# A gated DeltaNet's decay sums and key scales: as rows that a DMA spreads over the partitions, in place of a product and transposes on TensorE

## The reference

```python
gc = jnp.cumsum(g.reshape(B, N, C, H).transpose(0, 3, 1, 2), axis=-1)
decay = jnp.exp(jnp.where(incl, gc[..., :, None] - gc[..., None, :], -jnp.inf))
M = jnp.where(strict, jnp.einsum('bhncd,bhnjd->bhncj', kb, kc) * decay, 0.0)
A = jnp.eye(C, dtype=jnp.float32) + M
uw = lax.linalg.triangular_solve(A, rhs, left_side=True, lower=True, unit_diagonal=True)
qk = jnp.einsum('bhncd,bhnjd->bhncj', qc, kc) * decay
```

## Time and profile before

| | us |
|---|---|
| median of three runs | 1629.28 |
| lowest, highest | 1624.13, 1629.74 |
| the profiled execution's own time | 1627.18 |
| its span, first to last instruction | 1625.4 |
| PE busy in the span | 1592.6 (98%) |
| PE weight loads | 1327.0 (82%) |
| DVE busy | 883.1 (54%) |
| POOL busy | 648.7 (40%) |
| ACT busy | 578.5 (36%) |
| DMA, mean | 118 GB/s |
| share of PE in the chain that ended last | 91% |

### The profile page before, as it was taken

One profiled execution on the slowest core, in us unless ns is written; L12 is line 12 of the kernel. 1 busy time (PEld: TensorE's weight loads), 2 busy tenths in 40 slices (PEclk: granted clock), 3 DMA queues, 4 the chain that ended last, 5 costly groups with the idle time before them and its releaser, 6 DMA issues.

```text
span 1625.4 us, 20530 instructions
## 1 busy us (share of the span) xinstructions
PE 1592.6 (98%) x7955; PEld 1327.0 (82%) x7955; DVE 883.1 (54%) x1326; ACT 578.5 (36%) x838; POOL 648.7 (40%) x477
## 2 busy tenths in 40 slices
PE   7999999999999999999999999999999999999998
PEld 4888888888888888888788887788888888878886
DVE  5322222454536353566554148756666565878886
ACT  4422221123222243333222134444444444444445
POOL 3334322312131223224324347987788888000111
PEclk9999999999999999999999999999999999999999
DMA  5232332121213042335367031422234433686575
GB/s 171 66 94 88 115 97 61 43 69 39 69 38 81 27 125 71 99 113 154 122 209 269 14 110 35 135 91 91 91 98 122 124 108 94 232 306 218 195 263 183
DMA packets 204172, 192.24 MB, mean 118 GB/s; under 512 B 23364, under 2 KB 156972, under 8 KB 204076
## 3 DMA queue, kind: packets, MB, share of 16 engines
q1 hardware_dynamic: 203856, 190.85, 37.8%
q10 hardware_dynamic: 220, 0.09, 0.0%
HBM read 142.57 MB, written 48.33 MB: 117 GB/s over the span
## 4 chain that ended last, share of the span: by engine, by line
PE 91%; DVE 4%; DMA 2%; issue 1%; POOL 1%; SPq 1%; ACT 0%; DVEq 0%; ACTq 0%
PE acc L562 37%; PE acc L2469 12%; PE bank_ab L1408 7%; PE bank_ab L2469 6%; PE acc L2479 6%; PE att_ps L2469 5%; PE att_ps L2479 3%; PE bank_ab L2479 3%; PE acc L1843 3%; PE att_ps L1483 2%; PE bank_ab L1843 1%; PE att_ps L1843 1%; PE att_ps L1465 1%; DVE u_t_full L1799 1%; PE att_ps L1476 1%
## 5 line engine op out<-in xcount | busy, mean ns | idle before, releaser
L562 PE MATMUL acc<-xh,w_high 128*128 128x512 f32 x832 | 276.9, 409 | 0.6 <-POOL xl L1732 0.6
L562 PE MATMUL acc<-xl,w_high 128*128 128x512 f32 x832 | 262.1, 392 | 0.0
L562 PE MATMUL acc<-xh,w_low 128*128 128x512 f32 x832 | 261.1, 390 | 0.0
L973 POOL TENSOR_TENSOR w_low<-w_raw,w_high 128x1024 fp32r<-128x1024 f32 x49 | 117.4, 2395 | 346.8 <-ACT w_high L1055 346.8
L562 PEld LDWEIGHTS acc<-xh,w_low 128*128 128x128 f32 x832 | 156.5, 188 | 34.2
L562 PEld LDWEIGHTS acc<-xl,w_high 128*128 128x128 f32 x832 | 156.6, 188 | 33.9
L562 PEld LDWEIGHTS acc<-xh,w_high 128*128 128x128 f32 x832 | 147.2, 189 | 27.0 <-issue 3.8
L1146 ACT ACTIVATE sc<-sc,mx 128x128 f32<-128x128 f32 (+1 forms) x96 | 35.5, 441 | 173.4 <-DVE mx L1352 173.4
L1246 DVE SCALAR_TENSOR_TENSOR cs<-acc,prm,cs 128x1023 f32<-128x1023 f32 (+2 forms) x36 | 46.1, 1281 | 77.0 <-ACT cs L1073 76.2
L2245 POOL TENSOR_TENSOR f_h<-f_h,f_fw 128x512 f32<-128x512 f32 x8 | 10.9, 1368 | 175.1 <-ACT f_junk L2168 175.1
L2479 PE MATMUL acc<-f_w_high,f_gh 128*128 128x512 f32 x176 | 69.6, 395 | 3.5 <-DVE f_gl L2333 3.5
(11 more groups left out here) (386 smaller groups left out, 3828.1 us busy)
## 6 DMA issues: line engine op xcount, KB each, us to landing
w_raw<-in_w_in_dram SPq DMA_DIRECT2D x51, 512.0 KB, 4.6
f_raw<-glu_d SPq DMA_DIRECT2D x66, 256.0 KB, 3.1
f_raw<-in_w_down_dram SPq DMA_DIRECT2D x55, 256.0 KB, 4.0
w_raw<-in_w_up_dram SPq DMA_DIRECT2D x24, 512.0 KB, 5.2
glu_d<-u_free_high SPq DMA_DIRECT2D x22, 512.0 KB, 4.6
u_raw_even<-in_w_up_dram SPq DMA_DIRECT2D x20, 512.0 KB, 4.7
f_raw<-gsum_d SPq DMA_DIRECT2D x33, 256.0 KB, 3.5
conv_d<-so SPq DMA_DIRECT2D x16, 512.0 KB, 3.0
```

The source lines that it names most:

```text
L562: mm = nc.tensor.matmul(out[:, lo:hi], w, xx[:, lo:hi], start=first and j == 0, stop=last and j == 2)
L973: g.tensor_tensor(wl[:, n % 2], raw[:, n % 2], wh[:, n % 2].bitcast(F32), ALU.subtract).then_inc(s_wlo, 1)
```

## The change

The running sums and the factors `nbr` are made once for all chunks as rows: 32 partitions (chunk and head) by 128 positions. They are written to HBM (`rows_d`), and for each chunk one DMA reads them back with the same 1024 numbers to all 128 partitions (`spread`, 512 KB). With these rows the factor along the free axis is a plain multiply, so `kT` (PE and ACT) is gone, and `XB` is made from the keys as they were loaded; the decay exponent is mask minus row (POOL), plus a column that ACT adds as its bias, so the product with `Ls` and POOL's masking are gone. ACT's one exponential of 128x512 becomes four of 128x128, one for each head's bias. The sums count from the middle of the chunk (`Um`: minus one in the upper left), so no exponent grows large. Everything else stays in its place: where `kT` stood there is a `rest`.

```diff
 def dn_stages():
     def front(c):
-        return [[(name, c)] for name in ("kt", "kT", "kkD")]
+        return [[(name, c)] for name in ("kt", "kkD")]
...
-        out += [("vq", c)] + kt + [("P4", c)] + kT + [("T4", c)] + kkD + rest + [("P5", c)] + ml + [("T5", c)] + ob + sv0
+        out += [("vq", c)] + kt + [("P4", c)] + rest + [("T4", c)] + kkD + rest + [("P5", c)] + ml + [("T5", c)] + ob + sv0
...
+            if kind == "conv" and t == 3 * NH - 1 and k == 4:
+                items.append(("rowsT",))
...
-    use_b = {"kkD", "vq", "T4", "T5", "T6", "kS", "so"}
+    use_b = {"vq", "T4", "T5", "T6", "kS", "so"}
... SP
+            def load_spread(c):
+                if c:
+                    sp.wait_ge(s_gu, 2 * c - 1)
+                    sp.wait_ge(s_a, a_taken[("kt", c - 1)])
+                sp.dma_start(spread, rows_d[:, c, :].rearrange("j (h t) -> j h t", h=NH).unsqueeze(0)
+                             .to_broadcast([P, 2, NH, P])).then_inc(s_rl, 16)
+                if kind == "rowsT":
+                    sp.wait_ge(s_attk, att_no[("gatesum",)])
+                    sp.wait_ge(s_attk, att_no[it])
+                    for j in range(2):
+                        sp.dma_start(rows_d[j].rearrange("c (h t) -> (c h) t", t=P), rows_t[j][0:NT * NH, :]
+                                     ).then_inc(s_rst, 16)
                     if name == "load":
+                        sp.wait_ge(s_rst, 48)
+                        load_spread(0)
... (kkD, behind the eight stores of WT)
+                        if c + 1 < NT:
+                            load_spread(c + 1)
... POOL
+            step(g.tensor_copy(Um[:], U[:]))
+            step(g.tensor_scalar(Um[0:P // 2, :], U[0:P // 2, :], -1.0, None, ALU.add))
                     if name == "kt":
-                        g.tensor_tensor(DTr[:], bh(U[:]), bc(g_all[:, c, :]), ALU.mult).then_inc(s_gu, 1)
+                        g.tensor_tensor(DTr[:], bh(amask[:, 0:P]), spread[:, 0], ALU.subtract).then_inc(s_gu, 1)
                     if name == "kkD":
-                        pool.wait_ge(s_b, b_taken[(name, c)])
-                        g.tensor_tensor(DTr[:], DTr[:], bh(U[:]), ALU.mult).then_inc(s_dtm, 1)
-                        pool.wait_ge(s_dtm, 2 * c + 1)
+                        pool.wait_ge(s_gu, 2 * c + 2)
                         g.tensor_tensor(DTr[:], DTr[:], bc(rr[:, 1, :, c]), ALU.mult).then_inc(s_dtm, 1)
... ACT
                 if kind == "gatesum":
+                    g.activation(g_all[:].rearrange("p c h -> p (c h)"), att0[:, 3 * NT * NH:4 * NT * NH], ACT.Copy, scale=-1.0)
+                    g.activation(rows_t[0][0:NT * NH, :], att0[0:NT * NH, P:2 * P], ACT.Copy, scale=-1.0)
+                if kind == "rowsT":
+                    g.activation(rows_t[1][0:NT * NH, :], att0[0:NT * NH, 0:P], ACT.Copy).then_inc(s_attk, 1)
-                    if name == "kT":
-                        g.activation(XB[:], A4, ACT.Copy).then_inc(s_a, 1)
                     if name == "kkD":
-                        g.activation(DTr[:], B4, ACT.Exp).then_inc(s_b, 1)
+                        act.wait_ge(s_gu, 2 * c + 1)
+                        for h in range(NH):
+                            ins = g.activation(DTr[:, h, :], DTr[:, h, :], ACT.Exp, bias=g_all[:, c, h:h + 1])
+                        ins.then_inc(s_gu, 1)
... DVE
-                        g.tensor_tensor(XB[:], A4, bc(nbr[:, c, :]), ALU.mult)
+                        dve.wait_ge(s_rl, 16 * (c + 2))
+                        g.tensor_tensor(XB[:], ckqk[c % 2][:, NH:2 * NH, :], spread[:, 1], ALU.mult)
... PE
-                    for j, m in enumerate((U, Ls, ones)):
+                    for j, m in enumerate((U, Ls, ones, Um)):
+                    last = t_.matmul(att0[0:NT * NH, P:2 * P], g_all[:].rearrange("p c h -> p (c h)"), Um[:],
+                                     start=True, stop=True)
+                if kind == "rowsT":
+                    t_.matmul(att0[0:NT * NH, 0:P], nbr[:].rearrange("p c h -> p (c h)"), ident[:], start=True,
+                              stop=True).then_inc(s_atpe, 1)
-                    if name == "kT":
-                        last = each_head(A4, XB, None, True)
                     if name == "kkD":
-                        pe.wait_ge(s_a, a_taken[("kT", c)])
-                        pe.wait_ge(s_gu, c + 1)
-                        each_head(A4, kc, XB)
-                        last = t_.matmul(bank_b[:, :], Ls[:], DTr[:].rearrange("p h c -> p (h c)"), start=True,
-                                         stop=True)
+                        pe.wait_ge(s_a, a_taken[("kt", c)])
+                        last = each_head(A4, kc, XB)
```

More of the change, by code:

```diff
@@ L89, in dn_stages @@
     ml, sv0, sv1, sv2, ts, tl, ex = solving(0)
-    out = [("load", 0)] + rest * 3 + sum(front(0), []) + rest * 2 + ml + rest + sv0 + rest * 3 + sv1 + sv2 + rest
+    kt, kkD = front(0)
+    out = [("load", 0)] + rest * 3 + kt + rest + kkD + rest * 2 + ml + rest + sv0 + rest * 3 + sv1 + sv2 + rest
     out += ts + rest + tl + rest * 2 + ex + rest
     for c in range(NT):
-        kt, kT, kkD = front(c + 1) if c + 1 < NT else (rest, rest, rest)
+        kt, kkD = front(c + 1) if c + 1 < NT else (rest, rest)
         ml, sv0, sv1, sv2, ts, tl, ex = solving(c + 1) if c + 1 < NT else [[]] * 7
         ob = [("ob", c - 1)] if c else []
-        out += [("vq", c)] + kt + [("P4", c)] + kT + [("T4", c)] + kkD + rest + [("P5", c)] + ml + [("T5", c)] + ob + sv0
+        out += [("vq", c)] + kt + [("P4", c)] + rest + [("T4", c)] + kkD + rest + [("P5", c)] + ml + [("T5", c)] + ob + sv0
         out += [("P6", c)] + sv1 + [("kS", c)] + sv2 + ts + [("T6", c), ("vn", c)] + tl + [("so", c)] + ex
@@ L201, in build @@
     gsum_d = nc.dram_tensor("gsum_d", [FT, P, HALF], F32, kind="Internal").ap()
+    rows_d = nc.dram_tensor("rows_d", [2, NT, NH * P], F32, kind="Internal").ap()
     m_d = nc.dram_tensor("m_d", [NT, NBLK, NH, BASE, BASE], F32, kind="Internal").ap()
@@ L586, in mixer @@
     job_no = {(kind, t): n for n, (kind, t, _) in enumerate(jobs)}
-    use_a = {"kt", "kT", "kkD", "vq", "P4", "T4", "P5", "T5", "P6", "kS", "vn", "so", "ob"}
-    use_b = {"kkD", "vq", "T4", "T5", "T6", "kS", "so"}
+    use_a = {"kt", "kkD", "vq", "P4", "T4", "P5", "T5", "P6", "kS", "vn", "so", "ob"}
+    use_b = {"vq", "T4", "T5", "T6", "kS", "so"}
     dn = [it[1:] for it in items if it[0] == "dn" and it[1] not in OFF_PE]
@@ L594, in mixer @@
     b_taken = count([d for d in dn if d[0] in use_b])
-    att_no = count([it for it in items if it[0] in ("gates", "gatesum", "vT", "a_qk", "a_pT", "a_pv", "cmbT")])
+    att_no = count([it for it in items if it[0] in ("gates", "gatesum", "rowsT", "vT", "a_qk", "a_pT", "a_pv", "cmbT")])
     order = {it: n for n, it in enumerate(items)}
@@ L701, in mixer @@
             fold = sb(early, "fold", [P, 2 * NH])
+            rows_t = [sb(early, f"rows_t{j}", [P, P]) for j in range(2)]
         oh_at = ol_at + NBR * S * 4
@@ L708, in mixer @@
         stage_o = sb(ctx, "o_stage", [P, 2, NH, P])
+        Um = nc.alloc_sbuf_tensor_at("Um", [P, P], F32, offset=rows_at[-1])
+        spread = stage_o[:].rearrange("p a h c -> p (a h c)").rearrange("p (a h c) -> p a h c", a=2, h=NH)
         oh = nc.alloc_sbuf_tensor_at("g_oh", [P, NBR, S], F32R, offset=oh_at)
@@ L883, in x_sync @@
                     c = it[1]
+                    if c == 0:
+                        sp.wait_ge(s_gu, 2 * NT - 1)
+                        sp.wait_ge(s_a, a_taken[("kt", NT - 1)])
                     sp.wait_ge(s_obst, 16 * (c + 1))
```

19 lines of the change are left out of this document (9 added, 10 removed).

## The result

The changed kernel took 1617.36 us in the median of six runs (1615.18 to 1619.65), the kernel before 1627.78 us in six runs beside it (1624.13 to 1629.74). The ratio is 0.9942, with a 95% interval of 0.9932 to 0.9953: 10.4 us less. The forecast was 1617 us, the range 1610 to 1625. The profiled execution of the new kernel took 1619.19 us (span 1617.5), 8.0 us less than that of the kernel before.

The account below looks back on a forecast made before the run. PE was taken as the bound, busy 499.8 of 500 us from 200 to 700 us. 10.2 - 0.6 + 1.5 = 11.1 us less gave 1616.1 or 1618.2 us by two bases; forecast 1617, range 1610 to 1625.

Parts of the forecast that it names:

- The product: PE's float32 128x512 product with `Ls` in `kkD` goes, worth 0.88 us in each of eight chunks.
- Rival C: The slow first matmul comes with any float32 item, so the product is worth 0.46 us: 1620 us, chance 0.08.
- The transposes: PE's four transposes in `kT` go: 0.45 us in four chunks, 0.35 us in chunks 3 to 6.
- The small products: Two more PE products in `gatesum` and one in `rowsT` cost 0.6 us, bounds 0.4 to 1.4 us.
- The wait in chunk 7: PE's wait for DVE's first combination, queued behind `WT`, goes as `WT` comes sooner: 1.5 us less.
- The chain behind `kkD`: `WT` comes 3.5 to 4 us sooner in chunks 0, 1 and 7; even in chunks 2 to 6.
- The exponentials "at no cost": Four exponentials for one add at most 0.8 us per chunk on ACT, busy 144 of 500 us: no cost.
- The loads: Eight 512 KB spread loads, ahead of block load `m` in SP's queue: taken as 0, +3 us in the range.
- Rival B: Spread loads hold up block load `m`, stalling PE about 5 us in seven chunks: about 1651 us, chance 0.05.
- Rival A: DVE paces the combinations at 700 to 860 us, gain given back: about 1622 to 1627 us, chance 0.17.
- Shared access to SBUF: DVE's `XB` multiply, now with two SBUF inputs, held at most 2.4 us by POOL: taken as 0.
- Rival D: The clock, 0.97 in one 50 us window (1.5 us), may dip once more or never: within 2 us.

Follow-up runs that it names:

- e1: Changed kernel with the item `kT` kept (four transposes of `XB` on PE, ACT's copy), the product still out: 1620.50 us, ratio 0.9968.
- e2b: Changed kernel with the decay product kept on PE and the spread load issued behind the block load `m`: 1622.86 us, ratio 0.9977.
- e4: Kernel before without POOL's pass that multiplies the decay matrix by the mask, values not the reference's: 1623.21 us, ratio 0.9977.
- e10: e8 with DVE's attention combination `cmb` 5 moved behind `ob` 6, its PE transposes two places later: 1614.41 us, ratio 0.9922.
- e3: Changed kernel with one 128x512 exponential per chunk in place of four, column term left out, values not the reference's: 1617.76 us, ratio 0.9949.
- e8: Changed kernel with the four exponentials one place earlier on ACT, in the empty place `kT` left: 1615.51 us, ratio 0.9932.
- e6: Changed kernel with one spread load in place of eight, all chunks using chunk 0's rows, values not the reference's: 1618.60 us, ratio 0.9949.
- e9: e8 with the spread load issued behind the block load `m` in SP's queue: 1616.92 us, ratio 0.9943.
- e2: Changed kernel with the decay product kept on PE, one exponential and POOL's mask, spread load ahead of `m`: 1630.71 us, ratio 1.0027.
- e5: Changed kernel with two more 512 KB transfers behind each spread load, ahead of `m` in the queue: 1634.51 us, ratio 1.0047.
- e7: Changed kernel with DVE's `XB` multiply reading keys from PSUM, so one SBUF input, values not the reference's: 1618.99 us, ratio 0.9947.

## Why the prediction was right, and where it was off

- **The product, 0.88 us per chunk: right.** e1 shows 0.85 to 0.89. Rival C, 0.46 us, falls.
- **The transposes, 0.45 and 0.35 us: nearly.** e2b wins 0.40 to 0.49 us in each of the eight chunks, 3.7 us in all where the sum had 3.2. The 0.35 us taken for chunks 3 to 6, behind attention items, was about 0.1 us low.
- **The small products, 0.6 us: mis-sized, measured 1.2.** From the first small product of `gatesum` to what follows it are 55.28 - 54.04 = 1.24 us; before, 54.18 - 53.60 = 0.58 us. That is 0.66 us for two products, not 0.44, since they took 0.31 and 0.34 us, not 0.22. `rowsT` costs 0.33 us and about 0.2 for its edges. The bound of 1.4 us held.
- **The wait in chunk 7, 1.5 us: right,** by the trace after and by e4.
- **The chain behind `kkD`: right in kind.** The exponential of chunks 0, 1 and 7 starts ahead of PE's `kkD` (256.58 against 267.18 us in chunk 1). From the start of `kkD` to `WT` it is 1.09 us in chunks 0 and 1, where it was 5.2, and 2.17 in chunk 7, where it was 5.14: 4.1, 4.1 and 3.0 us sooner, where 3.5 to 4 were forecast. In chunks 2 to 6 it is 0.7 us sooner, not even.
- **`ckz`'s wait stays: right.** e10 shows that it could have been taken away as well. The prediction counts it to the work that combines attention outputs; `ckz` belongs to the DeltaNet's output and only stood behind that work.
- **The exponentials "at no cost": wrong, in one chunk.** ACT near 562 us:

```profile
562.60 1.27 ACT L1169 ACTIVATE d_DTr<-d_DTr,g_all 128x128 f32<-128x128 f32 x4
563.89 1.28 ACT L1133 ACT_TABLE_LOAD   x1
565.18 1.03 ACT L1133 ACTIVATE qk<-acc 128x1024 f32<-128x1024 f32 x1
566.10 1.05 ACT L1085 ACTIVATE w_high<-w_raw 128x1024 fp32r<-128x1024 f32 x1
567.05 1.01 ACT L1185 ACTIVATE PT<-att_ps 128x1024 f32<-128x1024 f32 x1
```

  Behind `PT` PE waits 1.08 us (568.12). The same chain before:

```profile
568.06 0.58 ACT L1137 ACTIVATE d_DTr<-bank_ab 128x512 f32<-128x512 f32 x1
...
571.82 1.02 ACT L1152 ACTIVATE PT<-att_ps 128x1024 f32<-128x1024 f32 x1
```

  It ended at 572.84, and PE took `PT` at 573.19: 0.35 us of room. The exponentials take 0.69 us longer. PE also came 0.69 us sooner against this chain, whose first link leads by 5.46 us (566.45 to 560.99) where PE would have led by 6.15. Together 0.69 + 0.69 - 0.35 = 1.03 us. e3 takes one of the two parts away and leaves 0.4, e8 takes the exponentials out of the chain and leaves none. In e1, which has the same exponentials, it is 1.09 us too. The share of busy time (144 of 500 us) said nothing about this: the question is what stands in ACT's queue ahead of a result for which PE comes just in time. With the 0.3 us for `O` this took 1.4 us back.
- **The loads, taken as 0: right, for the reason given.** In chunk 1 they took 3.5 us of the 4.1 us by which `m` came sooner. In e6 and e9 no cost of the rest is seen; e2 and e2b show what the same loads cost without the shorter chain. Rival B's threshold, a landing of some 15 us, was stated for the later chunks; chunk 1 has no room to spare. Its price, 35 us for a landing of 20 us, was not measured: in e5 `m` is issued up to 4.1 us later against PE's own progress, and that stalls three of the seven chunks that it counted.
- **Rival A, given back: falls.** The lead holds from 707 to 878 us.
- **Shared access to SBUF, taken as 0: right for `XB`.** The Trainium skill (GPSIMD Engine Reference, Specifications) has GpSimd and VectorE contend where VectorE has two SBUF inputs; e7 agrees, 1779 ns against 692, off the path. The operations that were on the path are others: the 12 columns ahead of `ckz` (2.36 us, in the kernel before too) and, where `m` is late, a multiply of the inversion (2.08 us in e2).

The terms as measured: 8 x 1.33 = 10.6, less 1.2 for small products and 1.4 for the waits in chunk 5, plus 1.5 for chunk 7, make 9.5; the forecast had 11.1. PE's first items also started 0.4 us later in the one profiled execution, and the lead of 8.95 us at 707 us is what they leave. The medians' difference of 10.4 us has an interval of 7.7 to 11.1 us, which holds the 9.5, so the 1 us between them may be no more than noise. That the median met the forecast of 1617 us to 0.4 us is in part luck: the sum was 1.6 us too large, and the forecast was set between two bases 2.1 us apart. The signs were off by as much: PE was busy for 8.0 us less in all (1592.6 to 1584.6), not 10, and for 99.7% up to 700 us, not 99.9%. Absolute times in two traces compare less well: the same item (transposes of `ckv`, chunk 0) starts between 248.87 us (e6) and 251.62 us (e7) in the profiled executions, so where two traces are compared, the lead that one has from the start is to be taken off first.

## What to carry to other kernels

Taking work from the busy engine gains its full price as long as nothing else is late; look through each queue for results that the busy engine takes with little room (0.35 us for `PT` here), since they hold no matter how idle their engine is. A large load put ahead of a small, urgent one in one queue costs nothing or turns the sign of the whole change, depending on how early the urgent one is issued: put it behind. Before a long chain is shortened at a cost, cut it once for the price of a pass to see in how many of its repetitions it is waited for; here it was one of eight. Where a wait stands behind small operations, look at what another engine runs beside them: ahead of the 2.3 us wait here stands one that took 2.36 us in place of 0.17.

## What the runs showed of the hardware beyond this

A wait of PE can cost more than its length. In e2 the matmuls behind the 3.95 us wait ran at a granted clock of 0.50 (1.2 GHz), where e2b had 1.00 (2.4 GHz); window, PE busy, clock, DMA share, GB/s:

```profile
285.00:290.00 5.00, 1.42 (x7) 0.97 0.21 52
290.00:295.00 5.00, 4.62 (x19) 0.50 0.01 3
295.00:300.00 5.00, 5.00 (x25) 0.85 0.11 27
```

Against e2b PE lost 7.06 us here: 3.95 of waiting, and 3.1 more. The wait of 2.3 us for `ckz` was followed by such a stretch in some traces and not in others with the same wait. First the changed kernel, then e8:

```profile
765.00:770.00 5.00, 2.74 (x14) 0.87 0.23 66
770.00:775.00 5.00, 5.00 (x25) 0.79 0.27 73
```

```profile
765.00:770.00 5.00, 3.47 (x20) 1.00 0.20 56
770.00:775.00 5.00, 5.00 (x32) 1.00 0.61 186
```

Of the twelve traces with this wait, six show a clock of 0.66 in the 5 us behind it, so part of them at 1.2 GHz (before, changed, e1, e3, e5, e9), and six show 1.00 (e2, e2b, e4, e6, e7, e8). In all twelve PE was busy for 7.7 of the 10 us before the wait's end. The stretch costs 1.5 us: the lead of e4 over the kernel before goes from 1.75 to 3.28 us across it, with no edit there. Of the five traces with the 1.1 us wait for `PT` (changed, e1, e5, e6, e7) one had it too (e6, 0.76 from 570 to 575 us), at 1.6 us. Whether a kernel has it in every execution isn't known, as only one was profiled of each. Rival D put this at 2 us either way.
